# Final norm of a hybrid mixer and expert layer: two of eight output tiles multiplied by GpSimd, the last expert's output taken earlier by VectorE

## The reference

```python
def rms_norm(x, g):
    xf = x.astype(jnp.float32)
    y = xf * lax.rsqrt(jnp.mean(xf * xf, axis=-1, keepdims=True) + EPS)
    return (y * g).astype(x.dtype)
...
    ye = jnp.einsum('becf,efd->becd', jax.nn.silu(a) * u, w_down) * gate[..., None].astype(h.dtype)
    scatter = lambda ib, yb: jnp.zeros((n_tok, d), yb.dtype).at[ib.reshape(-1)].add(yb.reshape(-1, d))
...
        x = x + g2 * expert_choice_ffn(h2, w_router[l], w_gate_e[l], w_up_e[l], w_down_e[l], cap_lat)
    return rms_norm(x, final_g)
```

## Time and profile before

| | us |
|---|---|
| median of 3 runs | 1749.31 |
| lowest and highest run | 1748.43, 1749.66 |
| profiled execution, its own time | 1748.36 |
| its span | 1746.4 |
| TensorE busy | 1668.2 (96% of the span) |
| VectorE busy | 1350.3 (77%) |
| ScalarE busy | 1046.7 (60%) |
| GpSimd busy | 146.2 (8%) |

### The profile page before, as it was taken

The page is one execution under the profiler, slowest core; times in us unless marked ns, Lnnn a source line. Parts: engine busy times, 40 slices in busy tenths (PEclk is TensorE's granted clock), DMA queues, the critical chain, the costliest instruction groups (busy, mean ns, idle before and its releaser), DMA issues.

```text
span 1746.4 us, 22137 instructions
## 1 busy us (share of the span) xinstructions
PE 1668.2 (96%) x8353; PEld 1382.7 (79%) x8361; DVE 1350.3 (77%) x1293; ACT 1046.7 (60%) x985; POOL 146.2 (8%) x137
## 2 busy tenths in 40 slices
PE   6999999999999379999999999999999999999995
PEld 3689987879888268888888888888888888888884
DVE  4566544318864788998899889989988998898897
ACT  5252221236641247777777777777777777777775
POOL 3002200002100010110100101101101001011010
PEclk9999999999999689999999999999999999999998
DMA  9216521111232669999999999999999999999996
GB/s 346 66 40 192 172 96 49 49 49 50 87 133 101 225 230 377 382 371 398 375 381 390 372 385 389 370 392 384 370 398 374 381 391 370 386 389 369 393 382 237
DMA packets 204441, 492.83 MB, mean 282 GB/s; under 512 B 5716, under 2 KB 18808, under 8 KB 204392
## 3 DMA queue, kind: packets, MB, share of 16 engines
q1 hardware_dynamic: 187616, 435.30, 66.9%
q0 software_dynamic: 13248, 47.09, 8.8%
q10 hardware_dynamic: 3528, 9.75, 1.4%
HBM read 471.07 MB, written 21.05 MB: 282 GB/s over the span
## 4 chain that ended last, share of the span: by engine, by line
PE 91%; DVE 5%; DMA 2%; ACT 1%; issue 0%; ACTq 0%; DVEq 0%; POOL 0%; POOLq 0%
PE ps L1124 88%; PE ps L1571 2%; DMA moda<-in_w_mod 1%; PE ps L1522 1%; DVE topi L2099 1%; DVE topv L2098 1%; DVE affT L2101 1%; DVE ring L2182 1%; PE ps L1459 0%; DVE wl L2149 0%; DMA xe<-ffn_in,idx_e 0%; PE ps L1143 0%; DVE wol L1981 0%; DVE ygT L1893 0%; DVE raw L1891 0%
## 5 line engine op out<-in xcount | busy, mean ns | idle before, releaser
L2149 DVE TENSOR_TENSOR wl<-ring,wh 128x2048 fp32r<-128x2048 f32 x384 | 877.4, 2289 | 104.8 <-ACT wh L1068 104.4
L1068 ACT ACTIVATE wh<-ring 128x2048 fp32r<-128x2048 f32 x384 | 737.1, 1921 | 279.4 <-PE ps L1124 279.4
L1124 PE MATMUL ps<-wh,xeh 128*128 128x512 f32 x1024 | 403.9, 394 | 0.3 <-DVE xel L2129 0.3
L1124 PE MATMUL ps<-wh,xel 128*128 128x512 f32 x1024 | 400.8, 391 | 0.0
L1124 PE MATMUL ps<-wl,xeh 128*128 128x512 f32 x1024 | 276.6, 392 | 0.0
L1124 PEld LDWEIGHTS ps<-wl,xeh 128*128 128x128 f32 x1024 | 192.4, 188 | 41.6
L1124 PEld LDWEIGHTS ps<-wh,xel 128*128 128x128 f32 x1024 | 192.5, 188 | 41.4
L1124 PEld LDWEIGHTS ps<-wh,xeh 128*128 128x128 f32 x1024 | 192.2, 188 | 40.7 <-DVE xel L2129 0.8
L1124 PE MATMUL ps<-wh,hidh 128*128 128x512 f32 x512 | 202.7, 396 | 0.0
L1124 PE MATMUL ps<-wh,hidl 128*128 128x512 f32 x512 | 200.1, 391 | 0.0
L1124 PE MATMUL ps<-wl,hidh 128*128 128x512 f32 x512 | 138.3, 392 | 0.0
(11 more groups left out here) (373 smaller groups left out, 2044.1 us busy)
## 6 DMA issues: line engine op xcount, KB each, us to landing
ring<-in_w_gate_e SPq DMA_DIRECT2D x64, 2048.0 KB, 9.2
ring<-in_w_up_e SPq DMA_DIRECT2D x64, 2048.0 KB, 9.0
ring<-in_w_down_e SPq DMA_DIRECT2D x64, 2048.0 KB, 10.5
mbw<-in_w_mod POOLq DMA_DIRECT2D x32, 512.0 KB, 5.1
hpr<-in_w_in SPq DMA_DIRECT2D x12, 1024.0 KB, 5.3
moda<-in_w_mod SPq DMA_DIRECT2D x3, 2048.0 KB, 20.2
xs<-in_x POOLq DMA_DIRECT2D x8, 512.0 KB, 8.4
wor<-in_w_out SPq DMA_DIRECT2D x2, 2048.0 KB, 7.7
```

Of the source, the lines that this page charges most:

```text
L1068: act.activation(whv[m % 4], eview(m), ACT.Copy).then_inc(hi_done, 1)
L1124: return pe.matmul(o, l, r, start=start, stop=stop)
L2149: dve.tensor_tensor(wlv[m % 4], eview(m), whv[m % 4].bitcast(F32), ALU.subtract).then_inc(lo_done, 1)
```

## The change

Three things change, all behind the last expert's last weights.

GpSimd takes tiles 3 and 5 (`BY_POOL`). For these VectorE gives only the reciprocal (`finv_ready`), and GpSimd multiplies the tile in place by `fgrow`, waits for that with its `link`, and multiplies it by the reciprocal, which is spread over the 1024 columns (`finp_ready`). SP waits for `finp_ready` ahead of the stores of these two tiles; the stores stay in the order of the tiles.

VectorE takes the last expert's output (scaling and sum) ahead of tiles 6 and 7 (`LATE`).

These two tiles go where VectorE waits for ScalarE: tile 6 ahead of the sum of the two halves' squares, tile 7 ahead of the last expert's reciprocal.

```diff
+    BY_POOL = (3, 5)
+    LATE = (6, 7)
...
+            pool.wait_ge(gains_in, 32)
+            for i, t in enumerate(BY_POOL):
+                pool.wait_ge(finv_ready, i + 1)
+                link(pool.tensor_tensor(finv[:, t, :], finv[:, t, :], fgrow[:], ALU.mult))
+                pool.tensor_tensor(finv[:, t, :], finv[:, t, :], stat[:, 2, t:t + 1].to_broadcast([P, D]),
+                                   ALU.mult).then_inc(finp_ready, 1)
             pool.wait_ge(out_in, 16 * NT)
             pool.wait_ge(tok_ready, 2)
...
             for t in range(NT):
-                sp.wait_ge(fin_ready, t + 1)
+                if t in BY_POOL:
+                    sp.wait_ge(finp_ready, BY_POOL.index(t) + 1)
+                else:
+                    sp.wait_ge(fin_ready, t + 1 - sum(b < t for b in BY_POOL))
                 sp.dma_start(out[0][t * P:(t + 1) * P, :], finv[:, t, :]).then_inc(out_in, 16)
...
             def final_scale(t):
                 dve.wait_ge(froot_ready, t + 1)
+                if t in BY_POOL:
+                    dve.reciprocal(stat[:, 2, t:t + 1], stat[:, 1, t:t + 1]).then_inc(finv_ready, 1)
+                    return
                 link(dve.reciprocal(stat[:, 2, t:t + 1], stat[:, 1, t:t + 1]))
...
             expert(NE - 1, False, True)
-            for t in range(EARLY, NT):
+            for t in range(EARLY, LATE[0]):
                 final_scale(t)
...
                 dve.tensor_tensor(tok[:, n * W:(n + 1) * W], tok[:, n * W:(n + 1) * W],
                                   yw[:, n * W:(n + 1) * W], ALU.add).then_inc(tok_sum, 1)
+            final_scale(LATE[0])
             dve.wait_ge(tok_sq, 2)
             dve.tensor_tensor(lastst[:, 1, 0:1], lastst[:, 0, 0:1], lastst[:, 0, 1:2], ALU.add).then_inc(tok_sq, 1)
+            final_scale(LATE[1])
             dve.wait_ge(tok_root, 1)
             link(dve.reciprocal(lastst[:, 2, 1:2], lastst[:, 2, 0:1]))
```

More of the change, by code:

```diff
@@ L412, in hybrid_block @@
         fin_ready = sem("fin_ready")
+        finv_ready = sem("finv_ready")
+        finp_ready = sem("finp_ready")
         out_in = sem("out_in")
```

## The result

The changed kernel takes 1751.99 us (median of 22 runs, lowest 1751.07), the kernel before 1748.95 in the same comparison (22 runs). The ratio is 1.0017 with a 95% interval of 1.0012 to 1.0023: about 3.0 us slower, 2.1 to 4.0. That is clear of zero and less than 0.2%. One of the 22 launches of the changed kernel took 1903.07 us at a granted clock of 0.84, against 0.98 in all others, and stands outside the ratio. The forecast was 1753.2 with a range of 1749.7 to 1754.9. The profiled execution took 1751.51 us with a span of 1749.7.

What follows compares the result with a forecast made beforehand. The chain to the last scatter, released by VectorE's last products, was taken to bound the kernel. With GpSimd and VectorE taking turns, the scatter comes 3.9 us later: 1749.31 + 3.9 = 1753.2 us, range 1749.7 to 1754.9.

Steps and rivals of the forecast that it cites:

- The limit: Tail: the scatter would follow the last store's landing, not the last products; token path gains 2.7 us, stores lose 4.2.
- the whole gain that was worked out: VectorE's tail: without hindrance the last products end at 1734.9, token path 2.7 us earlier, 0.15%.
- case 1: Tail: VectorE instructions with two SBUF inputs and GpSimd's products exclude each other, in turn; 3.9 us later, 1753.2; chance 0.58.
- The products: GpSimd's tiles 3 and 5: 2.05 us per product, 4.25 us per tile with 0.15 us wait.
- The sign set for this step: GpSimd's products: both kinds, alone on GpSimd, would show at 2.0 to 2.1 us.
- the doubt written beside it: GpSimd's products: a second input of full width, in place of a spread `cols`, could cost more; no size given.
- the gap ahead of the scatter: End of the chain: 0.77 us from the last condition to the scatter's start, the same in both kernels.
- case 2: Tail: no exclusion, the stores bound, 1.3 us later, 1750.6; chance 0.27.
- The other cases: Besides no exclusion: partial exclusion, near 1752, chance 0.11; cheap GpSimd products, 1747.6 at 1.0 us each, chance 0.04.

Runs made afterwards that it cites:

- e3_psum: Changed kernel with at most one SBUF tensor per VectorE tail instruction; ratio to the kernel before 1.0003, scatter T + 14.49 (T: start of tile 3's reciprocal).
- e4_memset: Changed kernel with GpSimd filling tiles 3 and 5 four times each with a constant instead of its products; not timed against before, scatter 0.28 us later than before.
- e5_one_tile: Changed kernel with GpSimd given tile 3 alone instead of tiles 3 and 5; ratio 1.0010 to the kernel before, scatter 1.60 us later.

## Why the prediction was right, and where its sizes were off

**The limit and the gain.** The chain's end was read rightly: GpSimd's tiles moved the limit from the last products to the landing of the stores. With the exclusion gone (e3_psum) the last products end at T + 9.9, 2.7 us earlier than before against T, the whole gain that was worked out.

**The exclusion, case 1.** It held, and in the order forecast: first product, tile 4, second, first sum, third, second sum, fourth, tile 6, tile 7. The evidence in the trace of before was one pair of selections, 1088 ns against 626, and I gave case 1 0.58. That pair was another kind of case, as told behind e4_memset: VectorE had a single tensor in SBUF there. So the trace of before spoke for turns between two instructions that the change doesn't contain, and could not tell what two SBUF inputs would do; that this evidence pointed the right way was in part luck. The Trainium skill's page "SBUF — State Buffer", section "Who interferes with whom", says that a VectorE instruction with two SBUF inputs contends with a GpSimd instruction that reads SBUF, not with one that only writes it. With at most one SBUF input, it says, the VectorE instruction does not contend outside the modes that use two ports; whether the scaling of the earlier trace rows ran in such a mode, no run here shows. The traces agree on all three points, GpSimd's read, its write, and a single input: 3.30 us in place of 1.28 in the changed kernel, 1.28 in e4_memset, 1.28 in e3_psum.

**The products.** I took 2.05 us each. Alone they take 2.40 and 2.35 by `fgrow` and 1.89 and 1.90 by the spread reciprocal (e3_psum). The pair was priced at 4.25 us with its wait, and takes 4.37. The sign set for this step, both kinds at 2.0 to 2.1 us, was thus not met by either; the doubt written beside it, that a second input of full width could cost more, was right. The 2.25 us that the prediction took from the Trainium skill's page "GPSIMD Engine Reference", section "Elementwise — side-by-side cycle accounting", is an estimate: half of a figure that the page gives for an addition of 2048 columns, not for a product. It lies between the two kinds. The row of `vw` has a spread second input as well, and fits the cheaper kind: 1.99 was worked out from it.

**Where 1.25 us of the sum went.** The forecast had the scatter 3.9 us later, T + 17.33; it came at T + 16.08. Four terms behind the third product carry that, all above the truth.

| step | forecast | measured | difference |
|---|---|---|---|
| third product ends | T + 8.27 | T + 8.29 | +0.02 |
| fourth product ends | T + 10.97 | T + 10.58 | -0.39 |
| tile 6's product ends | T + 12.17 | T + 11.66 | -0.51 |
| tile 7's product starts | T + 12.57 | T + 11.84 | -0.73 |
| last landing | T + 16.57 | T + 15.81 | -0.76 |
| scatter starts | T + 17.33 | T + 16.08 | -1.25 |

That the third product's end was met to 0.02 us is two errors cancelling, which is luck. The first product ends at T + 2.70 where T + 2.29 was forecast, but tile 4's product and the second of GpSimd take 2.84 us behind it, not 3.28. From the third to the fourth product's end I counted 2.70 us, 0.65 for the sum and 2.05 for the product, and it took 2.29: 0.54 and 1.75. The cheap kind explains 0.16 of that. The rest is that an instruction which has waited for its turn needs less behind the hand-over than it takes alone, 0.54 us against 0.69 for the sum and 1.75 against 1.89 for the product. So does tile 6's, which ends 1.08 us behind GpSimd's, where I counted 1.20. The small sum and tile 7's reciprocal take 0.18 us between two products, not 0.40, since the reciprocal begins under the sum. And the largest, 0.50 us, is the gap ahead of the scatter, which the prediction said was the same in both kernels. It was wrong to carry that row over: what comes last ahead of the scatter, and what GpSimd does before, differ.

**The chances.** The median rose by 3.0 us where 3.9 was forecast. The measured 0.17% lies within 0.2%, where 0.56 stood, while the single forecast of case 1 lay just above. With case 1 true, seven in ten of it were given to slower by over 0.2%; the 1.25 us of terms above put it below. The range is wide enough to hold case 2 as well (1750.6), so that it was met says little about the mechanism; the lengths in the traces and the experiments do. The other cases' prices held up where they could be run: case 2 (no exclusion) gave +1.3, e3_psum measured +1.04 with the gap at 0.27, that is 1.5 with the gap that was assumed.

## What to carry to other kernels

Before giving VectorE's work to GpSimd, count the SBUF tensors of what stays on VectorE beside it: with two there and a read on GpSimd's side, the engines take turns, and a tile that GpSimd norms in 4.4 us alone took 3.45 us from VectorE (e5_one_tile), which would have spent 1.39 us on it itself. One operand in PSUM lifted this here, for a copy by ScalarE that could be placed earlier. Then ask what stands in line behind the slower engine: here SP's stores in the order of the tiles cost 1 us that a turned order gave back, at no cost in work.

## What was not expected of the hardware

GpSimd's product with a second input spread from one column is faster than with a full one, 1.89 us against 2.40 for 128x1024. The gap between the last condition and an indirect transfer on GpSimd was 0.27 or 0.77 us, as told above. An instruction that waits for the other engine's turn is recorded as busy, not idle: VectorE's 3.30 us of tile 4's product are about 2 of waiting and 1.3 of work, and no view of waits names GpSimd for it. Only the length against its usual one shows it.
